# Gate and up weights of eight experts as pieces of 512 columns by half the contraction

## The reference

```python
D_MODEL, D_FF, N_EXPERTS, TOP_K = 1024, 3584, 8, 2

def swiglu(h, w_gate, w_up, w_down):
    return (jax.nn.silu(h @ w_gate) * (h @ w_up)) @ w_down

def moe_ffn(h, router_w, router_b, w_gate, w_up, w_down):
    t = h.reshape(bsz * seq, d)
    logits = t @ router_w + router_b
    top_v, top_i = lax.top_k(logits, TOP_K)
    gates = jax.nn.softmax(top_v, axis=-1)
    combine = jnp.sum(jax.nn.one_hot(top_i, N_EXPERTS) * gates[..., None], axis=1)
    out = jnp.zeros((bsz * seq, d))
    for e in range(N_EXPERTS):
        out = out + combine[:, e:e + 1] * swiglu(t, w_gate[e], w_up[e], w_down[e])
    return out
```

## Time and profile before

| | us |
|---|---|
| Median of 3 runs | 2600.26 |
| Lowest and highest | 2598.63 to 2601.04 |
| The profiled execution's own time | 2601.27 |
| Its span in the trace | 2599.5 |
| Mean granted TensorE clock | 0.963 |
| DVE busy | 1899.0 (73% of the span) |
| ACT busy | 1456.1 (56%) |
| Loaded from memory | 592.27 MB |

### The profile page before, as it was taken

The page is one execution under the profiler, slowest core; times in us unless marked ns, Lnnn a source line. Parts: engine busy times, 40 slices in busy tenths (PEclk is TensorE's granted clock), DMA queues, the critical chain, the costliest instruction groups (busy, mean ns, idle before and its releaser), DMA issues.

```text
span 2599.5 us, 39729 instructions
## 1 busy us (share of the span) xinstructions
PE 2479.1 (95%) x14992; PEld 2198.0 (85%) x14992; DVE 1899.0 (73%) x2063; ACT 1456.1 (56%) x1600; POOL 26.2 (1%) x47
## 2 busy tenths in 40 slices
PE   5999998899999999999999989998999999989998
PEld 5888888899999999999999968886888788767886
DVE  5676676688888888888888866677566766684765
ACT  3544444476767676767676754444544544544543
POOL 3000000000000000000000000000000000000000
PEclk8999999899999999999999989998899999987999
DMA  5555544598989899989898945532255455431552
GB/s 190 180 189 184 193 156 144 205 360 323 358 323 362 323 361 324 358 325 359 326 359 325 361 163 190 183 136 86 97 187 185 170 194 182 153 115 65 178 180 95
DMA packets 83808, 594.35 MB, mean 229 GB/s; under 512 B 9860, under 2 KB 10182, under 8 KB 12566
## 3 DMA queue, kind: packets, MB, share of 16 engines
q1 hardware_dynamic: 81216, 587.76, 63.3%
q0 software_dynamic: 1936, 4.44, 0.6%
q10 hardware_dynamic: 582, 1.16, 0.1%
HBM read 592.27 MB, written 1.05 MB: 228 GB/s over the span
## 4 chain that ended last, share of the span: by engine, by line
PE 89%; DVE 7%; ACT 2%; issue 1%; DMA 1%; ACTq 0%; DVEq 0%
PE banks L929 16%; PE banks L918 9%; PE banks L982 9%; PE banks L984 8%; PE banks L919 8%; PE banks L920 8%; PE banks L988 8%; PE banks L931 8%; DVE lo L1487 2%; PE banks L1211 2%; PE banks L958 2%; PE banks L1085 1%; DVE xhl L1564 1%; PE banks L1016 1%; PE banks L904 1%
## 5 line engine op out<-in xcount | busy, mean ns | idle before, releaser
L1487 DVE TENSOR_TENSOR lo<-raw,hi 128x2048 fp32r<-128x2048 f32 x550 | 1255.1, 2290 | 243.0 <-ACT hi L514 242.0
L514 ACT CAST hi<-raw 128x2048 fp32r<-128x2048 f32 x550 | 1052.3, 1914 | 180.5 <-PE banks L988 109.8
L929 PE MATMUL banks<-xhl,hi 128*128 128x512 f32 x1776 | 629.4, 398 | 1.2 <-DVE gsum L1518 1.2
L918 PE MATMUL banks<-hi,xhl 128*128 128x256 f32 x1952 | 564.7, 289 | 2.4 <-DVE lo L1487 1.6
L920 PE MATMUL banks<-hi,xhl 128*128 128x256 f32 x1952 | 553.0, 283 | 0.0
L919 PE MATMUL banks<-lo,xhl 128*128 128x256 f32 x1952 | 552.9, 283 | 0.0
L931 PE MATMUL banks<-xhl,lo 128*128 128x256 f32 x1776 | 498.5, 281 | 0.0
L929 PEld LDWEIGHTS banks<-xhl,hi 128*128 128x128 f32 x1776 | 333.6, 188 | 84.0 <-DVE lo L1487 1.6
L918 PEld LDWEIGHTS banks<-hi,xhl 128*128 128x128 f32 x1952 | 374.1, 192 | 14.3 <-issue 10.0
L919 PEld LDWEIGHTS banks<-lo,xhl 128*128 128x128 f32 x1952 | 374.7, 192 | 2.6
L920 PEld LDWEIGHTS banks<-hi,xhl 128*128 128x128 f32 x1952 | 374.2, 192 | 0.0
(11 more groups left out here) (355 smaller groups left out, 2427.7 us busy)
## 6 DMA issues: line engine op xcount, KB each, us to landing
raw<-in_moe_w_gate SPq DMA_DIRECT2D x112, 1024.0 KB, 4.9
raw<-in_moe_w_up SPq DMA_DIRECT2D x112, 1024.0 KB, 4.9
raw<-in_moe_w_down SPq DMA_DIRECT2D x112, 1024.0 KB, 4.9
raw<-in_ffn_w_gate SPq DMA_DIRECT2D x58, 1024.0 KB, 4.9
raw<-in_ffn_w_up SPq DMA_DIRECT2D x58, 1024.0 KB, 4.9
raw<-in_ffn_w_down SPq DMA_DIRECT2D x58, 1024.0 KB, 4.8
raw<-in_mix_pieces SPq DMA_DIRECT2D x46, 1024.0 KB, 4.8
raw<-in_mix_pieces SPq DMA_DIRECT2D x2, 768.0 KB, 4.1
```

What stands on the lines that cost most here:

```text
L514: nc.scalar.copy(hi[:, hslot(S, c), 0:n], raw[:, c % RING, 0:n]).then_inc(S.hi_done, 1)
L918: pe.matmul(o, xh[:, x0 + k, tk], hi[:, hr, wgt], start=(first and n == 0), stop=False)
L929: pe.matmul(bank[b + s][:, :], hi[:, hr, a:a + P], xhl[:, k, :], start=(k == 0), stop=False, skip_group_check=True)
L1487: v.tensor_tensor(lo[:, c % RING, 0:n], raw[:, c % RING, 0:n], hi[:, hslot(S, c), 0:n].bitcast(F32), ALU.subtract).then_inc(S.lo_done, 1)
```

## The change

The experts' gate and up weights are laid out on the host as pieces of 512 columns by half the contraction, still 1 MB each. A step now handles 512 inner channels with six pieces: two halves of the gate, two halves of the up and the two down pieces of the step before. There are 7 steps (STEPSW) for each expert, and the count of pieces stays at 336. Each gate or up piece is 12 products of 512 columns in place of 24 of 256 (`pe_wide`). SiLU, the product `hidden`, the rounding and the rest work on 128x512 in place of 128x256, half as often, and four blocks are turned at a time. The down pieces keep their layout.

The hand-written orders of the three engines are written anew. On ACT, SiLU stands behind the step's four gate and up copies; on DVE, `hidden` closes the step whose up product it reads, and the four gate and up subtractions come ahead of it. At an expert's start DVE does the subtractions of the four first pieces, then `hidden`, and then the next step.

```diff
+WIDE = 2 * FW
+STEPSW = F1 // WIDE
...
-            stage("moe", 0, 3 * STEPS1 * NE, STEPS1 * NE, n=STEPS1)
+            stage("moe", 0, 3 * STEPS1 * NE, STEPSW * NE, n=STEPSW)
...
+        def wide_at(B, m):
+
+            return B + 6 * m - 2 if m else B
+
+        def wide_rows_at(B, m):
+
+            return B + 6 * m + 8 if m < STEPSW - 1 else B + 6 * m + 4
...
+                def load(name, c, i, j):
+                    for r in range(2):
+                        sp_load(sp, S, c + r, i, w[name][e][:, bass.ds(2 * j + r, 1), :].rearrange("p j c -> p (j c)"), PIECE)
+
+                i0 = n * e
+                load("gate", B, i0, 0)
+                load("up", B + 2, i0, 0)
+                with sp.Fori(0, n - 1) as q:
+                    load("gate", wide_at(B, 1), i0 + q, q + 1)
+                    load("up", wide_at(B, 1) + 2, i0 + q, q + 1)
+                    load("down", wide_rows_at(B, 0), i0 + q, q)
+                load("down", wide_rows_at(B, n - 1), i0, n - 1)
 
         block = ctx.enter_context(nc.Block())
...
         def act_silu(act, S, c, i, t):
 
-            act.wait_ge(S.multiplied, c + 1 + 6 * i)
+            act.wait_ge(S.multiplied, c + 2 + 6 * i)
             act.wait_ge(S.hf_done, t)
-            nc.scalar.activation(sg[:, 0, :], bank[GATE][:, 0:FW], ACT.Silu).then_inc(S.sg_done, 1)
-
-        def act_round_h(act, S, c, i, t, turned0=0):
...
             def step(j, m, q):
-                act_silu(act, S, gate_at(B, m - 1), i0 + q, S0 + j - 1)
-                act_hi(act, S, gate_at(B, m), i0 + q)
-                act_hi(act, S, gate_at(B, m) + 1, i0 + q)
-                act_hi(act, S, rows_at(B, m - 1), i0 + q)
-                act_round_h(act, S, rows_at(B, m - 2), i0 + q, S0 + j - 1, st["S"])
+                c, r = wide_at(B, m), wide_rows_at(B, m - 1)
+                for n in range(4):
+                    act_hi(act, S, c + n, i0 + q)
+                act_silu(act, S, c, i0 + q, S0 + j)
+                act_hi(act, S, r, i0 + q)
+                if m > 1:
+                    act.wait_ge(S.multiplied, wide_rows_at(B, m - 2) + 2 + 6 * (i0 + q))
+                act_round_h(act, S, S0 + j - 1, st["S"])
+                act_hi(act, S, r + 1, i0 + q)
             return step
 
...
+            act_hi(act, S, B + 2, 0)
+            act_hi(act, S, B + 3, 0)
+            act_silu(act, S, B, 0, st["S"])
+            act_wide(act, S, st, 0)(1, 1, 0)
 
             def expert(e, last):
 
-                S0, i0 = st["S"] + n * e, n // 2 * e
-                step = act_step(act, S, st, e)
-                with act.Fori(0, n // 2 - 2) as q:
-                    step(2 + 2 * q, 2, q)
-                    step(3 + 2 * q, 3, q)
-                step(n - 2, n - 2, 0)
+                S0, i0 = st["S"] + n * e, n * e
+                step = act_wide(act, S, st, e)
+                with act.Fori(0, n - 3) as q:
+                    step(2 + q, 2, q)
                 act.wait_ge(S.pick_turned, e + 1)
                 nc.scalar.copy(pickT[:, :], bank[5][:, 0:T]).then_inc(S.pickT_done, 1)
                 step(n - 1, n - 1, 0)
-                act_silu(act, S, gate_at(B, n - 1), i0, S0 + n - 1)
-                act_hi(act, S, B + 3 * n - 1, i0)
+                r, i1 = wide_rows_at(B, n - 1), n * (e + 1)
+                act_hi(act, S, r, i0)
+                act_hi(act, S, r + 1, i0)
                 if not last:
-                    act_hi(act, S, B + 3 * n, i0)
                     act_gathered(act, S, e + 1, (0,))
-                act_round_h(act, S, rows_at(B, n - 2), i0, S0 + n - 1, st["S"])
+                act.wait_ge(S.multiplied, wide_rows_at(B, n - 2) + 2 + 6 * i0)
+                act_round_h(act, S, S0 + n - 1, st["S"])
                 if not last:
                     act_gathered(act, S, e + 1, (1,))
-                    act_hi(act, S, B + 3 * n + 1, i0)
-                act.wait_ge(S.multiplied, B + 3 * n + 6 * i0)
+                    for c in range(3):
+                        act_hi(act, S, B + c, i1)
+                act.wait_ge(S.multiplied, r + 2 + 6 * i0)
                 for b in range(2):
                     nc.scalar.copy(yh[:, 512 * b:512 * b + 512], bank[2 + b][:, :]).then_inc(S.yh_done, 1)
                 if not last:
-                    i1 = n // 2 * (e + 1)
-                    act_hi(act, S, gate_at(B, 1), i1)
+                    act_hi(act, S, B + 3, i1)
                     act_silu(act, S, B, i1, S0 + n)
-                    act_hi(act, S, gate_at(B, 1) + 1, i1)
-                    act_hi(act, S, rows_at(B, 0), i1)
-                    act_round_h(act, S, rows_at(B, -1), i1, S0 + n, st["S"])
...
+        def pe_wide(pe, S, c, i, bk, free):
+
+            for r in range(2):
+                pe.wait_ge(S.lo_done, split_no(S, c + r) + 1 + 6 * i)
+                if r == 0:
+                    pe.wait_ge(*free)
+                for n in range(4):
+                    k, wgt = 4 * r + n, slice(n * WIDE, n * WIDE + WIDE)
+                    h, o = hi[:, hslot(S, c + r), wgt], bank[bk][:, :]
+                    pe.matmul(o, xh[:, k, 0:P], h, start=(k == 0), stop=False)
+                    pe.matmul(o, xh[:, k, 0:P], lo[:, (c + r) % RING, wgt], start=False, stop=False)
+                    mm = pe.matmul(o, xl[:, k, 0:P], h, start=False, stop=(k == KD - 1))
+                mm.then_inc(S.multiplied, 1)
...
         def pe_up(pe, S, c, i, t):
-            pe_by_token(pe, S, c, i, UP, [(S.hf_done, t)]).then_inc(S.multiplied, 1)
...
+            pe_wide(pe, S, c + 2, i, UP, (S.hf_done, t))
...
-            for s in range(2):
-                mm = pe.transpose(bank[TURNED_H][:, s * P:s * P + P], hf[:, 0, s * P:s * P + P], ident[:, :])
+            for s in range(4):
+                mm = pe.transpose(bank[TURNED_H][:, s * P:s * P + P], flat(hf)[:, s * P:s * P + P], ident[:, :])
...
         def pe_step(pe, S, st, e):
-            B, S0, i0 = st["B"], st["S"] + st["n"] * e, st["n"] // 2 * e
+            B, S0, i0 = st["B"], st["S"] + st["n"] * e, st["n"] * e
 
             def step(j, m, q):
-                pe_gate(pe, S, gate_at(B, m), i0 + q, S0 + j)
+                pe_gate(pe, S, wide_at(B, m), i0 + q, S0 + j)
                 pe_turn_h(pe, S, S0 + j - 1)
-                pe_up(pe, S, gate_at(B, m) + 1, i0 + q, S0 + j)
+                pe_up(pe, S, wide_at(B, m), i0 + q, S0 + j)
                 pe.wait_ge(S.hl_done, S0 + j)
-                pe_rows(pe, S, rows_at(B, m - 1), i0 + q, hh, hl, 1)
+                pe_wide_rows(pe, S, wide_rows_at(B, m - 1), i0 + q)
             return step
...
             def expert(e, last):
 
-                S0, i0 = st["S"] + n * e, n // 2 * e
+                S0, i0 = st["S"] + n * e, n * e
                 step = pe_step(pe, S, st, e)
-                with pe.Fori(0, n // 2 - 2) as q:
-                    step(2 + 2 * q, 2, q)
-                    step(3 + 2 * q, 3, q)
+                with pe.Fori(0, n - 3) as q:
+                    step(2 + q, 2, q)
                 pe.wait_ge(S.added, 4 * e + 1)
                 for t in range(TT):
                     mm = pe.transpose(bank[5][:, t * P:t * P + P], pick[:, t, :].bitcast(F32), ident[:, :])
                 mm.then_inc(S.pick_turned, 1)
-                step(n - 2, n - 2, 0)
                 step(n - 1, n - 1, 0)
...
-            def step_of(S, st, e):
-                B, S0, i0 = st["B"], st["S"] + st["n"] * e, st["n"] // 2 * e
-
...
+                v.tensor_tensor(flat(hl), turned_h(), flat(hh).bitcast(F32), ALU.subtract).then_inc(S.hl_done, 1)
+
+            def wide_of(S, st, e):
+                B, S0, i0 = st["B"], st["S"] + st["n"] * e, st["n"] * e
+
+                def step(j, m, q, adds=None):
+                    c, r = wide_at(B, m), wide_rows_at(B, m - 1)
+                    for n in range(4):
+                        lo_piece(S, c + n, i0 + q)
+                    if adds:
+                        for b in range(3):
+                            adds(b)
+                    lo_piece(S, r, i0 + q)
                     rest_h(S, S0 + j - 1)
+                    lo_piece(S, r + 1, i0 + q)
+                    hidden(S, c, i0 + q, S0 + j)
+                    if adds:
+                        adds(3)
                 return step
 
...
+                lo_piece(S, B + 2, 0)
+                lo_piece(S, B + 3, 0)
+                hidden(S, B, 0, st["S"])
+                wide_of(S, st, 0)(1, 1, 0)
 
...
-                        step(3 + 2 * q, 3, q)
-                    step(n - 2, n - 2, 0)
+                    S0, i0 = st["S"] + n * e, n * e
+                    step = wide_of(S, st, e)
+                    with dve.Fori(0, n - 3) as q:
+                        step(2 + q, 2, q)
                     if not last:
                         dve.wait_ge(S.pick_turned, e + 1)
                         pick_of(S, pass_, e + 1)
                     step(n - 1, n - 1, 0)
-                    hidden(S, gate_at(B, n - 1) + 1, i0, S0 + n - 1)
```

(56 more changed lines are left out.)

54 lines of the change are left out of this document (22 added, 32 removed).

## The result

The changed kernel takes 2637.4 us (2636.9 to 2638.7) against 2600.4 for the kernel before: 1.0144 times as long, with a 95% interval of 1.0127 to 1.0160. It is slower by 37 us, far beyond the interval. The forecast was 2653, its range 2625 to 2680.

What follows compares the result with a forecast made beforehand. TensorE was taken to bound the expert stage. Against the profiled 2601.3 us: - 30 - 4 - 6 + 40 + 27 + 26 + 0.6 = + 53.6, 2655, rounded to 2653 for the median; range 2625 to 2680.

Steps and rivals of the forecast that it cites:

- What bounds the kernel: Expert stage: TensorE bounds it, nobody waits for a load; 14 steps are 122 of 128.9 us per expert.
- The products: 224 gate and up pieces: 12 products of 512 columns save 0.135 us a piece, 30 us less (27 to 34).
- Turning and the old stall: Turning four blocks at a time: 4 us less; TensorE's stall at an expert's first down piece goes: 6 us less.
- The wait at the pick table: Before the last step's gate piece: TensorE stalls 5.0 us, until W + 5.0 (W: turning's start), eight experts, 40 us more.
- The wait at an expert's start: DVE's `hidden` stands ahead of the next gate piece's low part: 3.3 us stall, eight starts, 27 us more.
- The clock: Slow products behind both stalls, 5 and 3 us, 3.7 us lost per expert: 26 us more (0 to 36).
- The steady step: Free: `hl` ends at 5.7 us, TensorE asks at 5.8, so it fits by 0.1 us.
- that rival: Clock holds at 1.00 through both stalls: + 27, 2627 us; chance 0.15.
- Loads: Rival: loads become the bound in the expert steps, six steps losing 0.6 us each, 29 us: 2682; chance 0.06.
- a waiting down piece: Rival: first down piece waits 0.3 us for `hl`, 48 times, adding 20 us: 2673; chance 0.08.
- products no faster: Rival: 512 columns cost twice 256 in gate and up pieces, + 30, 2683; chance 0.06.
- The other side: Rival: both waits are covered by copies already ready, only gains of 40 us are left: 2561; chance 0.05.

Runs made afterwards that it cites:

- both edits: Changed kernel with the pick-table copies two pieces later on ACT and DVE, and two low parts ahead of each expert's first `hidden` on DVE: 2555.1 us, ratio 0.9829.
- the run with halved products: Kernel with the two order edits, each 512-column gate or up product cut into two of 256: 2589.6 us; with one opening for the bank, 2587.7 us.
- the kernel with 1.72 us stalls: Changed kernel with pick-table copies later, plus 6 products of tables at rest behind the up product of an expert's first step: 2582.5 us, ratio 0.9935.

## Why the prediction was right, and where its sizes were off

- **What bounds the kernel.** Right. No engine waited for a load, before, after or with both edits, and TensorE's products followed each other without a pause in the steady steps; with both edits these drew 374 GB/s.
- **The products.** 30 us (27 to 34) were forecast, 32.5 measured. By the rule of the Trainium skill for a single product (TensorE: Matmul & The Clock Gate, Back-to-back issue gap) it would have been 7 us; the run with halved products disagrees with it and stands by the rows.
- **Turning and the old stall.** 10 us forecast; 12 are left over in the kernel with both edits, 1.5 of them the first expert's old wait. That the other 10.5 are the turning and the old stall is not shown one by one. The stall for `hl` at the first down piece is gone seven times, as said; the last expert's grew by 0.85 us (0.6 forecast).
- **The wait at the pick table.** Right in place, chain and size: W + 5.0 forecast, W + 5.04 measured, idle of 4.58 to 4.67 us, eight times. The old kernel with only the turning moved shows the same wait.
- **The wait at an expert's start.** Right as well: 3.3 us forecast with its slow first product, an idle of 3.11 measured, eight times (eight times 3.3 are 26, not 27; and 1.55 us of the first expert's stood there before). Both waits together: 67 us forecast, 65 measured as the difference of two runs.
- **The clock.** Right that the clock falls behind the stalls; the size was off, 26 us in the sum, 17 measured. The step put 5 us of slow products behind each long stall and 3 behind each short one, seven of eight times: 56 us. The trace has 28 us behind the long ones (35 forecast), since all but the first were followed by 3.1, and 10 behind the short ones (21 forecast), since six of eight were followed by none: 37 us. The price of 0.46 for each slow us held. The forecast treated each stall's clock as fixed by its own length; the runs show 0 to 6 us of slow products behind the same 3.11 us. The upper bound of 36 us stands there without a working.
- **The steady step.** 16.8 us forecast, 16.83 measured. In the step below, from the timelines of TensorE and DVE in the changed kernel, `hl` ends 5.65 us after the turning starts (5.7 forecast) and TensorE goes on to the down piece at 5.93 (5.8 forecast), without a wait: 0.28 us in hand where 0.1 was forecast.

```profile
1051.98 0.60 PE L1056 MATMUL banks<-ident,hf 128*128 128x128 f32 x4
...
1057.91 0.39 PE L1015 MATMUL banks<-hi,hh 128*128 128x512 f32 x1
```

```profile
1056.95 0.68 DVE L1543 TENSOR_TENSOR hl<-banks,hh 128x512 fp32r<-128x512 f32 x1
```

- **The sum.** 2655 on paper against a profiled 2638.7: 9 of the 16 us too much are the clock's, 2.5 the products', and the rest stands in parts of 2 us or less (the waits, the turning with the old stall, the stages behind).
- **The rivals.** The clock neither held nor fell everywhere; the time, 2637, lies between that rival's 2627 and the forecast. Loads, a waiting down piece and products no faster did not come. The Trainium skill (DMA: Bandwidth & Descriptors, Specifications) has about 358 GB/s for a core; steps here ran at 374. The other side, 2561 with both waits covered, needed two edits of order that the change did not have, and then took 2555.

## What to carry to other kernels

When steps are made longer, look at every instruction that stood "one step" ahead of its consumer: with half as many steps, one step of distance may have become none, and an in-order engine that waits for a product just made holds up the conversions queued behind it. Put what is needed next ahead of what merely becomes ready next; here two such exchanges turned 1.4% slower into 1.7% faster. And measure a clock cost by filling the idle with harmless products, or count the slow products in the trace; the number and length of the stalls do not give it. Taking one stall away shifts the others, and the slow stretches behind those can grow, as they did here from 10 to 44 us.

## What the runs showed of the hardware

- The clock's cost does not go by the length of the stall alone. A stall of 3.11 us in dense work was followed by 3.1 to 6.1 us of products at 1.2 GHz when it was the only long one in 130 us (1.6 to 2.5 us lost an expert, first products included), and by none in six of eight experts of the changed kernel. There a stall of 4.67 us stood some 43 us ahead of it; but in the second expert one stood 45 us ahead too, and 3.5 us of slow products followed.
- At an expert's start 1.72 us of idle left the clock at 1.00 eight times of eight; 2.41 us lowered it three times of eight; 3.11 us alone, and 4.67 us, every time. An idle of 1.83 us, ahead of the last expert's down piece in the kernel with both edits, was followed by 3.8 us of slow products, while one of the same length left the clock at 1.00 in the kernel with 1.72 us stalls; so 1.72 is not a safe length by itself.
- Products of 512 columns follow each other in 0.227 us, of 256 in 0.12: the half width is 5 to 6% dearer for the same columns, and a piece shows it as 2.72 against 2.87 us.
- In the kernel with both edits five slices of the page, 64 us long each, moved 372 to 375 GB/s, and no engine waited for a load in the expert stage.
